# Expert choice and the first up stage as one program, with a budget for the splits and 54 candidate pairs

## The chip, the cores and the metric

One core of a Trainium2 chip runs the whole kernel. The metric is the device time of one execution in microseconds. The page calls TensorE PE, VectorE DVE, ScalarE ACT, GpSimd POOL and SyncE SP.

## The reference, cut to what matters

Two blocks of two layers each work on 256 tokens of width 1024 in float32. The change touches only the expert layer (`peer_ffn`) of the second block, twice in an execution:

```python
q = (xc @ w_q).reshape(c, 8, 2, 128)
sc = jnp.einsum('chpd,hpnd->chpn', q, sub_keys)         # 8 heads, 2 halves, 128 keys each
top_s, top_i = lax.top_k(sc, 16)
cand_s = top_s[:, :, 0, :, None] + top_s[:, :, 1, None, :]      # 16 x 16 sums a head
cand_i = top_i[:, :, 0, :, None] * 128 + top_i[:, :, 1, None, :]
best_s, best_j = lax.top_k(cand_s.reshape(c, 8, 256), 16)
idx = jnp.take_along_axis(cand_i.reshape(c, 8, 256), best_j, axis=-1)
gate = jax.nn.softmax(best_s, axis=-1)
act = jax.nn.gelu(jnp.einsum('chkd,cd->chk', u_tab[idx], xc), approximate=False)
out = jnp.einsum('chk,chkd->cd', gate * act, v_tab[idx])
```

There are 128 x 128 experts with a row in `u_tab` and in `v_tab` each. Both lists of 16 are sorted, so the pair of the i-th best first and the j-th best second key (counted from 0) can be among the best 16 sums only where (i + 1)(j + 1) <= 16. The kernel before ignores this and selects among all 256 sums.

## The kernel before

**Dense experts.** The kernel gathers nothing. It multiplies the tokens by all of `u_tab` (the up stage, in two halves of 64 tiles of 128 experts: `up0` and `up1`), takes gelu of each, multiplies by a dense matrix of gates, and multiplies by all of `v_tab` (the down stage). A tile of 128 experts is one piece of 512 KB, loaded by SyncE into `w_raw` (four slots).

**Splits.** Each float32 weight is split in two parts for TensorE. A piece has two halves k = 2T and 2T + 1 for tile T. ScalarE copies a half to `w_hi` (`split_hi`, L182). VectorE subtracts it from the raw one to get `w_lo` (`split_lo`, L191). In `up0` VectorE does only the even halves and GpSimd the odd ones (`split_lo_too`, L200); each waits for the split before its own, so that the order of `w_lo_done` holds. `w_hi` and `w_lo` have four slots of one half each. TensorE then issues 12 matmuls a half (`col_half`, L224 to L226), 24 a tile, and ScalarE takes the gelu of each finished tile (L2667), which SyncE stores to HBM (L2610).

**Order in ScalarE's queue.** `UpPhase.scalar` splits both halves of tile T and then takes the gelu of tile T - 1. The two PSUM banks of the up products alternate, so TensorE's tile T waits for the gelu of tile T - 2.

**The choice.** `choose_experts` (L2914) is three programs (`nc.Block`), each of which ends on all engines before the next begins. The first is 64 matmuls of queries and keys on TensorE (L2946) and eight copies on ScalarE (L2955). The second runs `up0` on SyncE, TensorE, ScalarE and GpSimd, and the selection on VectorE: the best 16 of 128 keys in `top16` (MAX8 at L2997 and L3004, FIND_INDEX8 at L3000 and L3007, MATCH_REPLACE8 at L3001), two rows at a time; all 256 sums of a head (L3022) and `top16` over them; then the picks, which compare each chosen position with 0..15 in a tile of 128 x 16 (L3042), multiply by the key indices (L3046) and add up (L3050). VectorE's splits stand among these: `link` puts in one split at every second call and then waits for the operation before it. At the end ScalarE takes Exp of the scores (L3066) and VectorE normalizes (L3056 to L3060). The third program, `turn_heads`, transposes the three results (L847) and copies them to `chosen` (L855, L863). Then `up1` begins as a fourth program, in which VectorE makes one-hot rows out of `chosen`, does both halves of each split, and GpSimd none.

Of the kernel before, what the change touches and what calls it, by code (L numbers as in the profile page):

```python
# [2574 lines left out]
def passes(eng, body, rounds, peel_first=1, peel_last=False):  # L2575


    for n in range(peel_first):
        body(n)
    with eng.Fori(peel_first, rounds - peel_last) as n:  # L2580
        body(n)
    if peel_last:
        body(rounds - 1)
# [32 lines left out]
class UpPhase:  # L2616
# [41 lines left out]
    def scalar(self, act, gates=None):  # L2658
# [22 lines left out]
        passes(act, body, self.ROUNDS, peel_first=1 if self.which else 2)  # L2681
# [231 lines left out]

def choose_experts(K, qT, keys, iota16, chosen, phase):  # L2914
# [8 lines left out]
    V = nc.vector  # L2923
    with ExitStack() as ctx:
# [4 lines left out]
        topf = sb("top_index_f", [P, TT, HP, TOPK])  # L2929
        best = sb("best_scores", [P, TT, PH, TOPK])  # L2930
        bj = sb("best_index", [P, TT, PH, TOPK], U32)
        part = sb("best_part", [P, TT, 2, HK], U32)
        partf = sb("best_part_f", [P, TT, 2, HK])
        res = sb("chosen_rows", [P, TT, 3, HK])
        sm = sb("gate_sums", [P, TT, PH])
        exp_done = K.sem("gate_exp")
        scored, copied = K.sem("keys_scored"), K.sem("keys_copied")
        with ExitStack() as c2:
            ps = K.ps("key_scores_ps", [P, TT, HP // 4, 4, NK], c2)
            with nc.Block() as block:  # L2940
                @block.tensor
                def _(pe):
                    for t in range(TT):
                        for g in range(HP // 4):
                            for i in range(4):
                                ins = nc.tensor.matmul(ps[:, t, g, i, :], qT[:, 4 * g + i, t * P:(t + 1) * P],  # L2946
                                                       keys[:, 4 * g + i, :], start=True, stop=True)
                            ins.then_inc(scored, 1)

                @block.scalar  # L2950
                def _(act):
                    for t in range(TT):
                        for g in range(HP // 4):
                            act.wait_ge(scored, (HP // 4) * t + g + 1)
                            nc.scalar.activation(sc[:, t, 4 * g:4 * g + 4, :], ps[:, t, g], ACT.Copy).then_inc(copied, 1)  # L2955
        K.half_filled = 0

        def fill(dve):

            if K.half_filled < 2 * HALF:  # L2960

                if K.half_filled % 2 == 0:
                    K.split_lo(dve, phase.k0 + K.half_filled, in_turn=True)
                K.half_filled += 1

        def link(dve, ins):

            ins.then_inc(K.dve.sem, 1)
            K.dve.n += 1
            fill(dve)  # L2970
            dve.wait_ge(K.dve.sem, K.dve.n)

        with ExitStack() as c2:
            phase.take_banks(c2)
            rest = K.sb("scores_rest", [P, 2, NK], F32, c2)
            cand = K.sb("candidates", [P, 2, TOPK * TOPK], F32, c2)
            crest = K.sb("candidates_rest", [P, 2, TOPK * TOPK], F32, c2)
            eq = K.sb("picked", [P, HK, TOPK], F32, c2)
            with nc.Block() as block:
                @block.sync  # L2980
                def _(sp):
                    phase.sync(sp)

                @block.tensor
                def _(pe):
                    passes(pe, lambda n: [phase.tensor_tile(pe, j, n) for j in range(BODY)], phase.ROUNDS)

                @block.gpsimd
                def _(pool):
                    passes(pool, lambda n: [K.split_lo_too(pool, phase.k0 + 2 * j + 1, rep=n) for j in range(BODY)],  # L2990
                           phase.ROUNDS)

                def top16(dve, jobs):


                    for src, spare, v, i in jobs:
                        ins = V.max(v[:, 0:8], src)  # L2997
                    link(dve, ins)
                    for src, spare, v, i in jobs:
                        V.max_index(i[:, 0:8], v[:, 0:8], src)  # L3000
                        ins = V.match_replace(spare, v[:, 0:8], src, NEG_MAX)  # L3001
                    link(dve, ins)
                    for src, spare, v, i in jobs:
                        ins = V.max(v[:, 8:16], spare)  # L3004
                    link(dve, ins)
                    for src, spare, v, i in jobs:
                        ins = V.max_index(i[:, 8:16], v[:, 8:16], spare)  # L3007
                    return ins

                @block.vector  # L3010
                def _(dve):
                    for t in range(TT):
                        for g in range(HP // 2):
                            link(dve, top16(dve, [(sc[:, t, 2 * g + u, :], rest[:, u, :], top[:, t, 2 * g + u, :],
                                                   topi[:, t, 2 * g + u, :]) for u in range(2)]))
                    K.dve.link(dve, V.tensor_copy(topf[:], topi[:]))
                    for t in range(TT):
                        tv = top[:, t].rearrange("p (h a) k -> p h a k", a=2)
                        for h in range(0, PH, 2):
                            for u in range(2):  # L3020

                                ins = V.tensor_tensor(cand[:, u].rearrange("p (a b) -> p a b", a=TOPK),  # L3022
                                                      bcast_last(tv[:, h + u, 0, :], TOPK),
                                                      bcast_mid(tv[:, h + u, 1, :], TOPK), ALU.add)
                            link(dve, ins)
                            link(dve, top16(dve, [(cand[:, u], crest[:, u], best[:, t, h + u], bj[:, t, h + u])
                                                  for u in range(2)]))
                    for t in range(TT):
                        ins = V.tensor_tensor(res[:, t, 2, :].rearrange("p (h k) -> p h k", h=PH), best[:, t],
                                              bcast_last(best[:, t, :, 0], TOPK), ALU.subtract)  # L3030
                    ins.then_inc(exp_done, 1)
                    for t in range(TT):
                        flat = bj[:, t].rearrange("p h k -> p (h k)")
                        V.tensor_scalar(part[:, t, 0, :], flat, 4, None, ALU.logical_shift_right)
                        ins = V.tensor_scalar(part[:, t, 1, :], flat, 15, None, ALU.bitwise_and)
                    link(dve, ins)
                    link(dve, V.tensor_copy(partf[:], part[:]))
                    for t in range(TT):
                        tf = topf[:, t].rearrange("p (h a) k -> p h a k", a=2)
                        for a in range(2):  # L3040

                            link(dve, V.tensor_tensor(eq[:], bcast_last(partf[:, t, a, :], TOPK),  # L3042
                                                      bcast_mid(iota16, HK), ALU.is_equal))
                            for h in range(PH):
                                e = eq[:, h * TOPK:(h + 1) * TOPK, :]
                                ins = V.tensor_tensor(e, e, bcast_mid(tf[:, h, a, :], TOPK), ALU.mult)  # L3046
                                if h % 4 == 3:
                                    fill(dve)
                            link(dve, ins)
                            link(dve, V.tensor_reduce(res[:, t, a, :], eq[:], AX.X, ALU.add))  # L3050
                    while K.half_filled < 2 * HALF:
                        fill(dve)
                    dve.wait_ge(exp_done, 2)
                    g4 = lambda t: res[:, t, 2, :].rearrange("p (h k) -> p h k", h=PH)
                    for t in range(TT):
                        ins = V.tensor_reduce(sm[:, t, :], g4(t), AX.X, ALU.add)  # L3056
                    link(dve, ins)
                    link(dve, V.reciprocal(sm[:], sm[:]))
                    for t in range(TT):
                        V.tensor_tensor(g4(t), g4(t), bcast_last(sm[:, t, :], TOPK), ALU.mult)  # L3060

                @block.scalar
                def _(act):
                    phase.scalar(act)
                    act.wait_ge(exp_done, 1)
# [310 lines left out]
```

## Time and profile before

| | |
|---|---|
| median of 3 runs | 2782.22 us |
| lowest, highest | 2779.45, 2785.15 us |
| the profiled execution, its own time | 2781.84 us |
| its span | 2780.1 us |
| TensorE busy | 94% |
| VectorE busy | 74% |
| ScalarE busy | 54% |
| GpSimd busy | 8% |
| mean granted TensorE clock | 0.979 of full |

The span is what the profiler saw between the first and the last instruction; the execution's own time is what the metric counts. A share is an average over stages with different limits.

### The profile page before, as it was taken

How to read it: one execution, taken by the hardware profiler on the slowest of the kernel's cores; microseconds unless marked ns; L12 is line 12 of the kernel's file. 1: busy time of each engine (PE TensorE's matmuls, PEld its weight loads, DVE VectorE, ACT ScalarE, POOL GpSimd, SP SyncE). 2: the span in 40 equal slices, each digit the busy share in tenths (PEclk: the TensorE clock that was granted, in tenths of full speed). 3: DMA queues.
4: the chain of work that ended last, by engine and by line, in shares of the span. 5: the costliest groups of instructions: out<-in, count | busy, mean ns of one | idle time of the engine just before them, and what ended most of it. 6: DMA issues, size and time to landing. Idle time of an engine off the chain costs nothing. (4 is left out here: it accounts for less than half of the span.)

```text
span 2780.1 us, 56603 instructions
## 1 busy us (share of the span) xinstructions
PE 2620.0 (94%) x17192; PEld 2375.4 (85%) x17192; DVE 2045.2 (74%) x4601; ACT 1500.0 (54%) x2975; POOL 222.3 (8%) x172
## 2 busy tenths in 40 slices
PE   7989999989988999799999999989998999999997
PEld 6869988779976999799988888778998999888886
DVE  5767767767768569877767777786589777777777
ACT  6555555654555445466655555555454566555554
POOL 0000000000000044200000000000344000000000
PEclk9999999999999999999999999989999999999999
DMA  5226654236543477455567777625576555577775
GB/s 203 84 72 182 183 175 139 79 123 187 182 158 121 148 228 227 158 173 176 173 209 242 241 240 242 204 90 175 176 227 190 161 176 173 182 241 242 239 243 183
DMA packets 194609, 503.48 MB, mean 181 GB/s; under 512 B 22608, under 2 KB 88400, under 8 KB 193104
## 3 DMA queue, kind: packets, MB, share of 16 engines
q1 hardware_dynamic: 194512, 502.28, 57.4%
q8 instruction: 50, 0.82, 0.1%
q14 instruction: 47, 0.39, 0.0%
HBM read 467.59 MB, written 34.60 MB: 181 GB/s over the span
## 5 line engine op out<-in xcount | busy, mean ns | idle before, releaser
L191 DVE TENSOR_TENSOR w_lo<-w_raw,w_hi 128x512 fp32r<-128x512 f32 (+1 forms) x1432 | 975.8, 685 | 355.5 <-ACT w_hi L182 335.4
L182 ACT ACTIVATE w_hi<-w_raw 128x512 fp32r<-128x512 f32 (+2 forms) x1592 | 926.4, 621 | 179.3 <-PE banks_right L226 137.9
L224 PE MATMUL up_up<-hT_hi,w_hi 128*128 128x256 f32 x2048 | 596.4, 291 | 26.6 <-DVE w_lo L191 20.5
L225 PE MATMUL up_up<-hT_lo,w_hi 128*128 128x256 f32 x2048 | 582.1, 284 | 0.0
L226 PE MATMUL up_up<-hT_hi,w_lo 128*128 128x256 f32 x2048 | 582.0, 284 | 0.0
L224 PEld LDWEIGHTS up_up<-hT_hi,w_hi 128*128 128x128 f32 x2048 | 395.2, 193 | 31.2 <-DVE w_lo L191 23.9
L236 PE MATMUL banks_left<-w_hi,expert_hi 128*128 128x512 f32 x1008 | 393.7, 391 | 7.7 <-DVE w_lo L191 7.7
L225 PEld LDWEIGHTS up_up<-hT_lo,w_hi 128*128 128x128 f32 x2048 | 395.9, 193 | 0.0
L226 PEld LDWEIGHTS up_up<-hT_hi,w_lo 128*128 128x128 f32 x2048 | 395.1, 193 | 0.0
L237 PE MATMUL banks_left<-w_lo,expert_hi 128*128 128x512 f32 x1008 | 393.2, 390 | 0.0
L238 PE MATMUL banks_left<-w_hi,expert_lo 128*128 128x512 f32 x1008 | 393.1, 390 | 0.0
L200 POOL TENSOR_TENSOR w_lo<-w_raw,w_hi 128x512 fp32r<-128x512 f32 (+1 forms) x160 | 214.0, 1338 | 1941.6 <-POOLq L2895 608.7
L224 PE MATMUL banks_right<-hT_hi,w_hi 128*128 128x256 f32 x1120 | 325.9, 291 | 8.2 <-DVE hT_lo L573 2.9
L225 PE MATMUL banks_right<-hT_lo,w_hi 128*128 128x256 f32 x1120 | 320.8, 286 | 0.0
L226 PE MATMUL banks_right<-hT_hi,w_lo 128*128 128x256 f32 x1120 | 320.7, 286 | 0.0
L2667 ACT ACTIVATE expert_gelu<-up_up 128x256 f32<-128x256 f32 x256 | 98.4, 384 | 403.0 <-PE up_up L226 403.0
L2744 ACT ACTIVATE expert_hi<-gates 128x256 fp32r (+1 forms) x256 | 106.9, 418 | 323.6 <-PE banks_left L238 320.9
L224 PEld LDWEIGHTS banks_right<-hT_hi,w_hi 128*128 128x128 f32 x1120 | 218.8, 195 | 14.8 <-issue 5.9
L236 PEld LDWEIGHTS banks_left<-w_hi,expert_hi 128*128 128x128 f32 x1008 | 190.0, 189 | 47.5 <-DVE expert_lo L2760 8.1
L237 PEld LDWEIGHTS banks_left<-w_lo,expert_hi 128*128 128x128 f32 x1008 | 190.1, 189 | 39.6
L238 PEld LDWEIGHTS banks_left<-w_hi,expert_lo 128*128 128x128 f32 x1008 | 189.9, 188 | 39.3
L2760 DVE TENSOR_TENSOR expert_lo<-gates,expert_hi 128x256 fp32r<-128x256 f32 x256 | 109.0, 426 | 154.3 <-ACT expert_hi L2744 154.3
(400 smaller groups left out, 3890.8 us busy)
## 6 DMA issues: line engine op xcount, KB each, us to landing
w_raw<-in_peer_u_c SPq DMA_DIRECT2D x256, 512.0 KB, 3.5
w_raw<-in_peer_v SPq DMA_DIRECT2D x256, 512.0 KB, 3.5
w_raw<-in_w_up_c SPq DMA_DIRECT2D x88, 512.0 KB, 3.6
expert_gelu_held<-expert_gelu SPq DMA_DIRECT2D x256, 128.0 KB, 1.7
expert_back<-expert_gelu_held SPq DMA_DIRECT2D x256, 128.0 KB, 3.2
w_raw<-in_w_down SPq DMA_DIRECT2D x44, 512.0 KB, 4.1
w_raw<-in_w_in_r SPq DMA_DIRECT2D x40, 512.0 KB, 3.6
w_raw<-in_w_in_c SPq DMA_DIRECT2D x32, 512.0 KB, 3.6
```

The source lines that it names most:

```text
L182: self.nc.scalar.activation(self.w_hi[:, k % SLOTS, 0:width], self.raw_half(k, width), ACT.Copy).then_inc(self.sem("w_hi_done"), 1)
L191: self.nc.vector.tensor_tensor(self.w_lo[:, k % SLOTS, 0:width], self.raw_half(k, width), self.w_hi[:, k % SLOTS, 0:width].bitcast(F32), A ...
L200: self.nc.gpsimd.tensor_tensor(self.w_lo[:, k % SLOTS, 0:width], self.raw_half(k, width), self.w_hi[:, k % SLOTS, 0:width].bitcast(F32), A ...
L224: self.nc.tensor.matmul(bank, hi, self.hT_hi[:, c, :], start=(c == 0), stop=False)
L225: self.nc.tensor.matmul(bank, hi, self.hT_lo[:, c, :], start=False, stop=False)
L226: last = self.nc.tensor.matmul(bank, lo, self.hT_hi[:, c, :], start=False, stop=(c == DC - 1))
L236: self.nc.tensor.matmul(bank, act_hi[:, cols], hi, start=start, stop=False)
L237: self.nc.tensor.matmul(bank, act_hi[:, cols], lo, start=False, stop=False)
L238: last = self.nc.tensor.matmul(bank, act_lo[:, cols], hi, start=False, stop=stop)
L2667: K.nc.scalar.activation(shelf.out[:, j, :], self.up[:, j % 2, 0:SEQ], ACT.Gelu).then_inc(self.gelu_done, 1)
L2744: K.nc.scalar.activation(self.hi[:, j % 2, :], tile_of(self.gates, j + BODY * n), ACT.Copy).then_inc(self.hi_done, 1)
L2760: self.K.nc.vector.tensor_tensor(self.lo[:, j % 2, :], tile_of(self.gates, j + BODY * n), self.hi[:, j % 2, :].bitcast(F32), ALU.subtract) ...
```

## The change

The first two programs of `choose_experts` and the transposes become one program, beside `up0`:

- TensorE computes the scores of tokens 0 to 127, tile 0 of `up0`, the scores of tokens 128 to 255 in the same banks (each group after ScalarE's copy of the first), and then the other tiles. Ahead of tile 63 it waits for the gates and does the six transposes.
- ScalarE copies the scores after the splits of tile 0 and, for the second half, after those of tile 1 and the first gelu. Exp stands behind the gelu of tile 55, in the iteration of tile 56.
- VectorE's splits are placed by a budget (`Paced`): each operation counts 0.13 us + width/950, and a split is put in as soon as 1.9 us are reached, behind the operation that was just issued and ahead of the wait for it. After the picks the splits up to the 58th (tile 57) follow, then the normalization, then the last six, and the copies to `chosen`.
- `top16` works on four rows at a time. The second selection works on 54 sums a head, laid out in five segments (rows 0; 1; 2 to 3; 4 to 7; 8 to 15 with 16, 8, 5, 3, 1 columns). The place of a chosen one among the 54 is turned into row and column by 20 operations on 128 x 256.
- The picks become 16 times `(part == k) * index[k]` on 128 x 512 (scalar_tensor_tensor) and 15 additions, each waiting for the one before.
- `passes` can leave out more than one last iteration of the loop; ScalarE peels two and TensorE one.

The removed lines are those of the program above.

```diff
@@ -2579,8 +2579,8 @@
         body(n)
     with eng.Fori(peel_first, rounds - peel_last) as n:
         body(n)
-    if peel_last:
-        body(rounds - 1)
+    for n in range(rounds - peel_last, rounds):
+        body(n)
 def is_first(n):
@@ -2655,7 +2655,7 @@
         for j in range(BODY):
             store(j, self.ROUNDS - 1)
-    def scalar(self, act, gates=None):
+    def scalar(self, act, gates=None, also={}, peel_last=0):
         K, k0, shelf = self.K, self.k0, self.shelf
         def gelu(j, n):
@@ -2678,7 +2678,9 @@
                     gates.move(act, j - 2, n)
                 elif gates and not is_first(n):
                     gates.move(act, j + 2, n - 1)
-        passes(act, body, self.ROUNDS, peel_first=1 if self.which else 2)
+                if isinstance(n, int) and (n, j) in also:
+                    also[n, j]()
+        passes(act, body, self.ROUNDS, peel_first=1 if self.which else 2, peel_last=peel_last)
         gelu(BODY - 1, self.ROUNDS - 1)
         if gates:
             for j in (2, 3):
@@ -2911,6 +2913,43 @@
     phase.end()
+class Paced:
+    def __init__(self, K, dve, phase, each):
+        self.K, self.dve, self.k0, self.each = K, dve, phase.k0, each
+        self.spent, self.filled = 0.0, 0
+    def fill(self):
+        if self.filled < HALF:
+            self.K.split_lo(self.dve, self.k0 + 2 * self.filled, in_turn=True)
+            self.filled += 1
+    def fill_to(self, count):
+        while self.filled < count:
+            self.fill()
+    def spend(self, width, ops=1):
+        self.spent += ops * (0.13 + width / 950)
+        while self.spent >= self.each:
+            self.spent -= self.each
+            self.fill()
+    def link(self, ins, width, ops=1):
+        self.K.dve.mark(ins)
+        self.spend(width, ops)
+        self.K.dve.settle(self.dve)
+SEGMENTS = [(0, 1, 16), (1, 2, 8), (2, 4, 5), (4, 8, 3), (8, 16, 1)]
+CAND_N = sum((b - a) * w for a, b, w in SEGMENTS)
+FIRST_OF_ROW = [0, 16, 24, 29, 34, 37, 40, 43, 46]
+assert all(any(a <= i < b and j < w for a, b, w in SEGMENTS) for i in range(TOPK) for j in range(TOPK) if (i + 1) * (j + 1) <= TOPK)
 def choose_experts(K, qT, keys, iota16, chosen, phase):
@@ -2921,152 +2960,165 @@
     NEG_MAX = -3.0e38
     HK = PH * TOPK
     V = nc.vector
+    EXP_AT, TAIL = (phase.ROUNDS - 2, 0), 58
     with ExitStack() as ctx:
         sb = lambda n, s, d=F32: K.sb(n, s, d, ctx)
         sc = sb("key_scores", [P, TT, HP, NK])
         top = sb("top_scores", [P, TT, HP, TOPK])
         topi = sb("top_index", [P, TT, HP, TOPK], U32)
...
+        topf = sb("top_index_f", [P, TT, 2, PH, TOPK])
         best = sb("best_scores", [P, TT, PH, TOPK])
         bj = sb("best_index", [P, TT, PH, TOPK], U32)
...
+        partf = sb("best_part_f", [P, TT, 2, PH, TOPK])
+        term = sb("picked_term", [P, TT, 2, PH, TOPK])
+        picked = sb("picked", [P, TT, 2, PH, TOPK])
+        gate = sb("chosen_gates", [P, TT, HK])
         sm = sb("gate_sums", [P, TT, PH])
...
+        rest = sb("scores_rest", [P, 4, NK])
+        cand = sb("candidates", [P, TT, PH, CAND_N])
+        crest = sb("candidates_rest", [P, 4, CAND_N])
+        pos = sb("best_position", [P, TT, PH, TOPK])
+        row, line, first = (sb(f"best_{n}", [P, TT, PH, TOPK]) for n in ("row", "line", "first"))
+        scored, copied, exp_done, ready, turned = (
+            K.sem(n) for n in ("keys_scored", "keys_copied", "gate_exp", "chosen_ready", "chosen_turned"))
+        phase.take_banks(ctx)
+        ps = K.ps("key_scores_ps", [P, HP // 4, 4, NK], ctx)
+        tps = K.ps("chosen_ps", [P, 4, SEQ], ctx)
+        with nc.Block() as block:
+            @block.sync
+            def _(sp):
+                phase.sync(sp)
+            @block.tensor
+            def _(pe):
+                def scores(t):
+                    for g in range(HP // 4):
+                        if t:
+                            pe.wait_ge(copied, g + 1)
+                        for i in range(4):
+                            ins = nc.tensor.matmul(ps[:, g, i, :], qT[:, 4 * g + i, t * P:(t + 1) * P],
+                                                   keys[:, 4 * g + i, :], start=True, stop=True)
+                        ins.then_inc(scored, 1)
+                def turn():
+                    pe.wait_ge(ready, 1)
+                    for j in range(3):
+                        for t in range(TT):
+                            src = gate[:, t, :] if j == 2 else picked[:, t, j]
+                            ins = nc.tensor.transpose(tps[:, j, t * P:(t + 1) * P], src, K.ident[:])
+                        if j:
+                            ins.then_inc(turned, 1)
+                def body(n):
+                    for j in range(BODY):
+                        if isinstance(n, int) and n == phase.ROUNDS - 1 and j == BODY - 1:
+                            turn()
+                        phase.tensor_tile(pe, j, n)
+                        if is_first(n) and j == 0:
+                            scores(1)
+                scores(0)
+                passes(pe, body, phase.ROUNDS, peel_last=1)
+            @block.gpsimd
+            def _(pool):
+                passes(pool, lambda n: [K.split_lo_too(pool, phase.k0 + 2 * j + 1, rep=n) for j in range(BODY)],
+                       phase.ROUNDS)
+            @block.scalar
+            def _(act):
+                def copies(t):
+                    for g in range(HP // 4):
+                        act.wait_ge(scored, (HP // 4) * t + g + 1)
+                        nc.scalar.activation(sc[:, t, 4 * g:4 * g + 4, :], ps[:, g], ACT.Copy).then_inc(copied, 1)
+                def gates():
+                    act.wait_ge(exp_done, 1)
+                    nc.scalar.activation(gate[:], gate[:], ACT.Exp).then_inc(exp_done, 1)
+                phase.scalar(act, also={(0, 0): lambda: copies(0), (0, 1): lambda: copies(1), EXP_AT: gates}, peel_last=2)
+            @block.vector
+            def _(dve):
+                pace = Paced(K, dve, phase, 1.9)
+                link = pace.link
+                def top16(jobs):
+                    n = jobs[0][0].shape[-1]
                     for src, spare, v, i in jobs:
                         ins = V.max(v[:, 0:8], src)
...
+                    link(ins, n, len(jobs))
                     for src, spare, v, i in jobs:
                         V.max_index(i[:, 0:8], v[:, 0:8], src)
                         ins = V.match_replace(spare, v[:, 0:8], src, NEG_MAX)
...
+                    link(ins, n + 70, 2 * len(jobs))
                     for src, spare, v, i in jobs:
                         ins = V.max(v[:, 8:16], spare)
...
+                    link(ins, n, len(jobs))
                     for src, spare, v, i in jobs:
                         ins = V.max_index(i[:, 8:16], v[:, 8:16], spare)
...
+                    link(ins, n + 70, len(jobs))
+                pace.fill()
+                for t in range(TT):
+                    for g in range(0, HP, 4):
+                        dve.wait_ge(copied, (HP // 4) * t + g // 4 + 1)
+                        top16([(sc[:, t, g + u, :], rest[:, u, :], top[:, t, g + u, :], topi[:, t, g + u, :])
+                               for u in range(4)])
+                for t in range(TT):
+                    ins = V.tensor_copy(topf[:, t].rearrange("p a h k -> p h a k"), topi[:, t].rearrange("p (h a) k -> p h a k", a=2))
+                link(ins, 256, 2)
+                for t in range(TT):
+                    tv = top[:, t].rearrange("p (h a) k -> p h a k", a=2)
+                    c0 = 0
+                    for a, b, w in SEGMENTS:
+                        n = (b - a) * w
+                        ins = V.tensor_tensor(cand[:, t, :, c0:c0 + n].rearrange("p h (a b) -> p h a b", b=w),
+                                              bcast_last(tv[:, :, 0, a:b], w), bcast_mid(tv[:, :, 1, 0:w], b - a), ALU.add)
+                        pace.spend(PH * n)
+                        c0 += n
+                K.dve.link(dve, ins)
+                for t in range(TT):
+                    for h in range(0, PH, 4):
+                        top16([(cand[:, t, h + u], crest[:, u], best[:, t, h + u], bj[:, t, h + u]) for u in range(4)])
+                for t in range(TT):
+                    ins = V.tensor_tensor(gate[:, t].rearrange("p (h k) -> p h k", h=PH), best[:, t],
+                                          bcast_last(best[:, t, :, 0], TOPK), ALU.subtract)
+                ins.then_inc(exp_done, 1)
+                pace.spend(128, 2)
+                link(V.tensor_copy(pos[:], bj[:]), 256)
+                link(V.tensor_scalar(line[:], pos[:], FIRST_OF_ROW[8] - 1.0, 0.0, ALU.subtract, ALU.max), 256)
+                for s in FIRST_OF_ROW[1:8]:
+                    src = line if s == FIRST_OF_ROW[1] else row
+                    link(V.scalar_tensor_tensor(row[:], pos[:], float(s), src[:], ALU.is_ge, ALU.add), 256)
+                for i, (a, b, w) in enumerate(SEGMENTS):
+                    c = float(FIRST_OF_ROW[a] - w * a)
+                    link(V.tensor_scalar((line if i else first)[:], row[:], float(w), c, ALU.mult, ALU.add), 256)
+                    if i:
+                        link(V.tensor_tensor(first[:], first[:], line[:], ALU.min), 256)
+                V.tensor_copy(partf[:, :, 0], row[:])
+                link(V.tensor_tensor(partf[:, :, 1], pos[:], first[:], ALU.subtract), 256, 2)
+                flat = lambda x: x.rearrange("p t a h k -> p (t a h) k")
+                value = lambda k: bcast_last(flat(topf)[:, :, k], TOPK)
+                for k in range(TOPK):
+                    dst = term if k else picked
+                    link(V.scalar_tensor_tensor(flat(dst), flat(partf), float(k), value(k), ALU.is_equal, ALU.mult), 512)
+                    if k:
+                        link(V.tensor_tensor(picked[:], picked[:], term[:], ALU.add), 512)
+                pace.fill_to(TAIL)
+                dve.wait_ge(exp_done, 2)
+                g4 = lambda t: gate[:, t, :].rearrange("p (h k) -> p h k", h=PH)
+                for t in range(TT):
+                    ins = V.tensor_reduce(sm[:, t, :], g4(t), AX.X, ALU.add)
+                link(ins, 128, 2)
+                link(V.reciprocal(sm[:], sm[:]), 16)
+                for t in range(TT):
+                    ins = V.tensor_tensor(g4(t), g4(t), bcast_last(sm[:, t, :], TOPK), ALU.mult)
+                ins.then_inc(ready, 1)
+                pace.fill_to(HALF)
+                for i in range(2):
+                    dve.wait_ge(turned, i + 1)
+                    rows = slice(2 * i, min(2 * i + 2, 3))
+                    V.tensor_copy(chosen[:, rows, :], tps[:, rows, :])
+        phase.end()
 def second_layer(K, l, cols, table, after, entry, following):
```

## Rows read from the trace of the kernel before

**Rows 1.** The page, part 1: busy us, share of the span, instructions.
```profile
PE 2620.0 (94%) x17192; PEld 2375.4 (85%) x17192; DVE 2045.2 (74%) x4601; ACT 1500.0 (54%) x2975; POOL 222.3 (8%) x172
```

**Rows 2.** Stretches, first layer: window, length, busy us of each engine; clock, DMA.
```profile
963.35:1117.80 154.45, 154.38 (x1272) 154.17 (x1272) 123.54 (x459) 77.27 (x160) 68.77 (x53) 0.99 0.71 222
1117.80:1160.60 42.80, 34.27 (x264) 32.49 (x264) 39.46 (x51) 14.80 (x31) 18.17 (x11) 1.00 0.50 159
```

**Rows 3.** TensorE's timeline at both edges: start, length, operation, idle before it.
```profile
953.50 7.38 PE L2946 MATMUL key_scores_ps<-sub_keys,peer_qT 128*128 128x128 f32 x64 [0.78 <-PEq L618]
963.35 0.43 PE L224 MATMUL up_up<-hT_hi,w_hi 128*128 128x256 f32 x1 [2.46 <-DVE w_lo L191]
...
966.98 0.28 PE L226 MATMUL up_up<-hT_hi,w_lo 128*128 128x256 f32 x1
...
1160.32 0.28 PE L226 MATMUL up_up<-hT_hi,w_lo 128*128 128x256 f32 x1
1164.38 1.01 PE L847 MATMUL chosen_ps<-ident,chosen_rows 128*128 128x128 f32 x6 [3.78 <-PEq L2979]
1167.62 0.58 PE L224 MATMUL up_up<-hT_hi,w_hi 128*128 128x256 f32 x1 [2.23 <-DVE w_lo L191]
```

**Rows 4.** ScalarE's timeline at both edges and at tile 53, SyncE's last stores.
```profile
960.92 0.60 ACT L2955 ACTIVATE key_scores<-key_scores_ps 128x512 f32<-128x512 f32 x1 [0.30 <-PE key_scores_ps L2946]
961.86 2.19 ACT L182 ACTIVATE w_hi<-w_raw 128x512 fp32r<-128x512 f32 x4 [0.34 <-PEq L2940]
...
968.01 0.39 ACT L2667 ACTIVATE expert_gelu<-up_up 128x256 f32<-128x256 f32 x1 [2.66 <-PE up_up L226]
...
1117.76 0.38 ACT L2667 ACTIVATE expert_gelu<-up_up 128x256 f32<-128x256 f32 x1 [1.37 <-PE up_up L226]
...
1160.64 0.38 ACT L2667 ACTIVATE expert_gelu<-up_up 128x256 f32<-128x256 f32 x1 [2.52 <-PE up_up L226]
1161.04 1.28 ACT L3066 ACT_TABLE_LOAD   x1
1162.33 0.42 ACT L3066 ACTIVATE chosen_rows<-chosen_rows 128x256 f32<-128x256 f32 x1
...
1159.25 2.13 SPq L2610 DMA_DIRECT2D expert_gelu_held<-expert_gelu  x4
```

**Rows 5.** Waits, 1116 to 1162, then 2114 to 2162: total us, times, longest.
```profile
PE up_up L224 <- DVE w_lo L191: 5.5, 6, 2.0
PE up_up L224 <- POOL w_lo L200: 3.1, 2, 1.5
...
PE up_up L224 <- DVE w_lo L191: 5.6, 6, 2.0
```

**Rows 6.** VectorE's and GpSimd's timelines in the picks, VectorE's ahead of `up1`.
```profile
1114.59 3.27 DVE L3042 TENSOR_TENSOR picked<-best_part_f,iota 128x2048 f32<-128x2048 f32 x1
1117.78 0.68 DVE L191 TENSOR_TENSOR w_lo<-w_raw,w_hi 128x512 fp32r<-128x512 f32 x1
1118.38 3.87 DVE L3046 TENSOR_TENSOR picked<-picked,top_index_f 128x256 f32<-128x256 f32 x8
...
1125.57 2.28 DVE L3042 TENSOR_TENSOR picked<-best_part_f,iota 128x2048 f32<-128x2048 f32 x1
...
1166.87 0.69 DVE L191 TENSOR_TENSOR w_lo<-w_raw,w_hi 128x512 fp32r<-128x512 f32 x1 [1.02 <-ACT w_hi L182]
...
1114.38 1.33 POOL L200 TENSOR_TENSOR w_lo<-w_raw,w_hi 128x512 fp32r<-128x512 f32 x1 [1.66 <-DVE w_lo L191]
1118.62 1.34 POOL L200 TENSOR_TENSOR w_lo<-w_raw,w_hi 128x512 fp32r<-128x512 f32 x1 [2.91 <-DVE w_lo L191]
...
1125.80 3.16 POOL L200 TENSOR_TENSOR w_lo<-w_raw,w_hi 128x512 fp32r<-128x512 f32 x1 [1.50 <-DVE w_lo L191]
```

**Rows 7.** VectorE's groups by form (first layer's choice): busy us, mean ns; one line's instructions.
```profile
L3000 DVE FIND_INDEX8 top_index<-top_scores,key_scores 128x8 uint32<-128x128 f32 x32 | 9.1, 286 | 0.0
...
L473 DVE SCALAR_TENSOR_TENSOR x<-x,banks_right x8: 632/680/689, 890.6 to 1894.5; 128x512 f32<-128x512 f32 x8
```

More of the change, by code:

```diff
@@ L2928, in choose_experts @@
         topi = sb("top_index", [P, TT, HP, TOPK], U32)
-        topf = sb("top_index_f", [P, TT, HP, TOPK])
+        topf = sb("top_index_f", [P, TT, 2, PH, TOPK])
         best = sb("best_scores", [P, TT, PH, TOPK])
         bj = sb("best_index", [P, TT, PH, TOPK], U32)
-        part = sb("best_part", [P, TT, 2, HK], U32)
-        partf = sb("best_part_f", [P, TT, 2, HK])
-        res = sb("chosen_rows", [P, TT, 3, HK])
+        partf = sb("best_part_f", [P, TT, 2, PH, TOPK])
+        term = sb("picked_term", [P, TT, 2, PH, TOPK])
@@ L2935, in choose_experts @@
+        picked = sb("picked", [P, TT, 2, PH, TOPK])
+        gate = sb("chosen_gates", [P, TT, HK])
         sm = sb("gate_sums", [P, TT, PH])
[L2936 to L2993, printed above, removed]
@@ L2996, in top16 @@
                     for src, spare, v, i in jobs:
                         ins = V.max(v[:, 0:8], src)
-                    link(dve, ins)
+                    link(ins, n, len(jobs))
                     for src, spare, v, i in jobs:
@@ L3001, in top16 @@
                         ins = V.match_replace(spare, v[:, 0:8], src, NEG_MAX)
-                    link(dve, ins)
+                    link(ins, n + 70, 2 * len(jobs))
                     for src, spare, v, i in jobs:
                         ins = V.max(v[:, 8:16], spare)
-                    link(dve, ins)
+                    link(ins, n, len(jobs))
                     for src, spare, v, i in jobs:
                         ins = V.max_index(i[:, 8:16], v[:, 8:16], spare)
-                    return ins
@@ L3010, in _ @@
[L3010 to L3065, printed above, removed]
-                    nc.scalar.activation(res[:, :, 2, :], res[:, :, 2, :], ACT.Exp).then_inc(exp_done, 1)
-            phase.end()
-        with ExitStack() as c2:
-            turn_heads(K, c2, "chosen", [(lambda t, j=j: res[:, t, j, :]) for j in range(3)], chosen)
+                    link(ins, n + 70, len(jobs))
[5 more added lines that the diff above has]
+                               for u in range(4)])
```

## The prediction

> **What bounds the kernel now.** I read the page's busy shares first: TensorE is busy 94% of the span [rows 1], so only stretches in which it stands still or runs slow can be won. The stretches by engine show where, in the choice with the first up stage of the first of two equal layers: up to 1117.8 us it never stands still, and from there to 1160.6 us it is busy 34.3 of 42.8 us while VectorE is nearly full [rows 2]. Then TensorE's timeline for the edges [rows 3], ScalarE's and SyncE's for the steps between two programs [rows 4], the waits for the late stretch [rows 5], and the timelines of VectorE and GpSimd there [rows 6].
>
> From the first key score (953.50) to the first matmul of the second up stage (1167.62) are 214.1 us [rows 3]. They add up so:
> - key scores: 7.38.
> - 960.88 to 963.35, waiting for the first split: 2.47.
> - After that pause the matmuls come 0.21 apart, at 1.2 GHz; the eighteenth (966.98) is the first at 0.12, 2.4 GHz: 3.63 us for what takes 17 x 0.12 = 2.04, so 1.59 lost.
> - 64 tiles of 24 matmuls at 0.12: 184.3. The gelus, one a tile, confirm it: 52 periods from 968.01 to 1117.76 are 2.88 each [rows 4].
> - the last 11 periods, 1117.76 to 1160.64, are 42.88 instead of 31.68: 11.2 lost, waiting for w_lo from VectorE and GpSimd [rows 5].
> - last matmul issued by 1160.44, next stage at 1167.62: 7.18 (last gelu, a program's end, Exp, the gate sums, a program's end, transposes of 1.01, again an end, first split).
> Sum 214.1. The second layer waits the same [rows 5].
>
> **What the change takes away, per layer.** Key scores of the first half run at once, and the split of tile 0 beside them: VectorE and GpSimd have 3.7 us for 0.7 + 1.3 [rows 6]. The second half's scores follow tile 0, whose 2.88 us cover ScalarE's copies. So the 2.47 go, and with no pause ahead of tile 0 its 1.59 too. The scores' own 7.38 stay on TensorE. Exp and gate sums leave the end. What is left after the last tile: last matmul's issue to gelu's end 0.20 + 0.38, SyncE's store issue 0.34 (its row ends 1161.38, the gelu 1161.02), the program's end 0.34 (961.52 to 961.86), first w_hi to w_lo 0.66, w_lo to matmul 0.75 (1166.87 to 1167.62) [rows 3, 4, 6]: 2.7, against 7.18, and the six transposes now stand ahead of tile 63 as 1.01 more. The slow start of the second up stage stays, since 2.5 us of pause were enough for it at 963.35. Gone: 2.47 + 1.59 + 7.18 - 2.7 - 1.0 = 7.5. Gone too, if the splits are in time: the 11.2. Together 18.7.
>
> The 54 candidates instead of 256, the four jobs a step and the new arithmetic cost or save nothing by themselves: until 1117.8 TensorE didn't wait for VectorE. They matter through when a split is late.
>
> **When a split is late.** In steady state the w_hi of tile T+1 is done about 1.1 us after tile T-1 ends (0.20 to the gelu, its 0.38, w_hi 2.19/4 = 0.55 [rows 4]) and VectorE's split must start by 2.88 - 0.69 - 0.07 = 2.1. VectorE may so be 1.0 us late. The program puts a split behind each 1.9 us of its own estimate, 0.13 + width/950 an operation (below: the budget), a split takes 0.60 (1117.78 to 1118.38 [rows 6]): 2.5 of 2.88, which looks safe. First selection: 32 rows of two MAX8, two FIND_INDEX8 and a replace over 128, five records, each read as the 0.286 of a FIND [rows 7], 1.43 x 32 = 46 us at most, against a budget of 8 groups x 6.18 = 49.4, so 26 splits: 46 + 26 x 0.6 = 62 us beside 75 us of TensorE. It is covered, and without that cover each us late would be a us lost. Over 54 the 16 rows take between 54/128 of that and the same, 10 to 23 us; with 9.7 splits 16 to 29 beside 28 us, and I take 22, since part of each is fixed. At joints, where eight FIND and replace operations stand between two splits (8 x 0.286 = 2.3 us at most), I put 0.5 us.
>
> The rest of the selection is another kind of work. The index arithmetic is 20 operations on 256 elements, the picks 16 + 15 on 512, nearly all with two inputs in SBUF, and GpSimd does the other half of each split. The rows say that these exclude each other: the 2048-wide comparison takes 2.28 us alone but 3.27 where a GpSimd split had begun; a GpSimd split that came while it ran took 3.16 instead of 1.33; eight multiplications by 256 took 3.87 where by width they are worth 2.28, and a GpSimd split is most of the difference [rows 6]. So a tile costs VectorE 0.60 (split) + 1.33 (GpSimd) + the budget's operations. By the budget a pick is 0.669, so 2.84 of them a split. A two-input operation of 512 records 0.68 (read from a scalar_tensor_tensor of that width whose one input was in PSUM [rows 7]), and each waits for the one before. With one of three starting while GpSimd waits its turn I take 0.65 each: 1.85. Sum 3.78, 0.90 more than 2.88. The picks' budget, 31 x 0.669 = 20.7, is 10.9 splits: 9.8 us lost. The index part, 20 x 0.40 = 8.0 us of budget, is 4.2 splits: 3.8, less the 1.0 that VectorE may be late, less 1.0 as an estimate for its operations with one input, which are worth less than budgeted: 1.8. Sum 11.6. The added waits (one after nearly each operation) hold up only what is in that sum: the next split, hence GpSimd's, hence TensorE.
>
> The Trainium skill states the rule that this speaks for: SBUF — State Buffer, section "SBUF: two separate sides", has VectorE's operations with two SBUF inputs and GpSimd's share a port pair as an exclusive lock, held for the whole instruction. The trace agrees (3.16 for 1.33). By 1.9 + 0.6 < 2.88 alone the change would look free of late splits; by the rule it is not.
>
> Exp in the middle: after gelu 55 ScalarE loads a table and does Exp, 1162.33 - 1161.04 + 0.42 = 1.71 us [rows 4]; tile 57's split is that much later, less 1.0 of slack: 0.7 lost. The gelu table's reload, 1.29, fits: ScalarE works 1.5 of each 2.88. Bounds 0 to 2. VectorE and the transposes aren't late: budget 100 us / 1.9 = 53 splits, so the picks end near tile 54, and the gates are due before tile 63, 17 us of margin even after waiting for Exp in tile 56.
>
> The Trainium skill, ScalarE: Activation LUTs, section "What ACT_TABLE_LOAD costs", adds a drain of about 1.38 us to the load's 1.28. The trace shows 1.29 from load to Exp, with the engine already empty; by the page this step would lose 1.4 us more a layer, and the estimate would be 2773.
>
> **Sum.** Lost anew: 11.6 + 0.5 + 0.7 = 12.8 of 18.7. Won 5.9 a layer, 11.8 in two. The profiled execution took 2781.8 (span 2780.1), 0.4 below the median 2782.2, so I leave that aside: 2770. Unknown ends: the picks' loss from 0 (no exclusion for scalar_tensor_tensor, short waits) to 18 (each 0.2 us dearer and GpSimd 0.3 later); joints 0 to 2. If only some terms err, 2762 to 2777.
>
> **Rivals.**
> A. The splits are in time after all: the picks are chained with gaps, and GpSimd works in them or isn't excluded by the new operation. Then only 0.7 to 2 are lost, 17 to 18 won a layer: 2747. For it: the rows show only operations in unbroken series or 2048 wide, and no scalar_tensor_tensor beside GpSimd. Against: the 3.16 and 3.87, and that the other half of the picks are additions of the kind shown.
> B. Slower. GpSimd doesn't get its turn between two operations of VectorE but after three: its half comes 1.83 later (3.16 - 1.33), so TensorE waits some 1.8 us in each of 15 tiles: 27 + 1.2 lost against 18.7, 19 slower in two layers: 2801. It decides from 1.2 us a tile on. Against: at 1118.62 GpSimd began after the first of eight multiplications with no gap between them [rows 6].
> C. The picks are dearer than read (each add and compare 0.2 us longer): 31 x 0.2 = 6.2 more a layer and nothing is left: 2781, no change.
>
> **How the numbers follow.** Forecast 0.62, A 0.2, C 0.1, B 0.08. The range holds the forecast's 2762 to 2777 and most of A, and leaves out B and the lowest of A: 2748 to 2779. A measurement here tells 0.2%, 5.6 us, from no change. Faster by more: the forecast's (less 0.05 for its upper end) and A's, and nothing of C: 0.78 to 0.84, taken as 0.82. Within: 0.1. Slower: 0.08.
>
> **What would show it.** TensorE: no pause between scores and tile 0, matmuls 0.12 apart from the start; about 2.7 us between up stages. Gelu periods of 2.88 up to about tile 38, then near 3.8 for some 12 tiles, 2.88 again with one longer by 0.7 at tile 57. GpSimd's split records near 1.8 in the picks. If the periods stay 2.88 there, A holds; if they pass 4.1, B or C. The forecast is wrong also if a wait stands ahead of the transposes.

## The result and the profile after

The changed kernel takes 2762.14 us (median of 4 runs, 2759.4 to 2765.01), the kernel before 2780.9 beside it. The ratio is 0.9926, 95% interval 0.9914 to 0.9938: faster by 0.6% to 0.9%. The forecast was 2770, 11.8 us won; 18.8 were. The profiled execution is the slowest of the four: 2765.01, span 2763.2.

TensorE's timeline at the edges of the first layer's stage, as in [rows 3]:

```profile
956.74 3.81 PE L2999 MATMUL key_scores_ps<-sub_keys,peer_qT 128*128 128x128 f32 x32 [0.78 <-PEq L618]
960.31 0.36 PE L224 MATMUL up_up<-hT_hi,w_hi 128*128 128x256 f32 x1
960.51 0.28 PE L225 MATMUL up_up<-hT_lo,w_hi 128*128 128x256 f32 x1
960.63 0.28 PE L226 MATMUL up_up<-hT_hi,w_lo 128*128 128x256 f32 x1
...
963.27 3.74 PE L2999 MATMUL key_scores_ps<-sub_keys,peer_qT 128*128 128x128 f32 x32
...
1154.39 0.60 PE L3008 MATMUL chosen_ps<-ident,picked 128*128 128x128 f32 x4
1154.82 0.38 PE L3008 MATMUL chosen_ps<-ident,chosen_gates 128*128 128x128 f32 x2
1160.74 0.39 PE L224 MATMUL up_up<-hT_hi,w_hi 128*128 128x256 f32 x1 [2.67 <-DVE w_lo L191]
```

No pause stands between the scores and tile 0, and its matmuls come 0.12 apart from the start. From the first score to the next up stage are 204.0 us, 214.1 before. (That the stage begins 3.2 later than before is not the change's: it was there before any changed instruction ran. From the first gelu of the second up stage to the next layer's first score it is 0.9 longer as well, 781.3 instead of 780.4. So the two profiled spans differ by 16.9 only, though the two layers' stages give more.)

ScalarE's timeline: a late stretch, Exp, the last gelu:

```profile
969.91 0.38 ACT L2667 ACTIVATE expert_gelu<-up_up 128x256 f32<-128x256 f32 x1 [1.24 <-PE up_up L226]
...
1073.61 0.38 ACT L2667 ACTIVATE expert_gelu<-up_up 128x256 f32<-128x256 f32 x1 [1.46 <-PE up_up L226]
...
1124.87 0.38 ACT L2667 ACTIVATE expert_gelu<-up_up 128x256 f32<-128x256 f32 x1 [1.41 <-PE up_up L226]
...
1133.51 0.38 ACT L2667 ACTIVATE expert_gelu<-up_up 128x256 f32<-128x256 f32 x1 [1.46 <-PE up_up L226]
1133.91 1.28 ACT L3035 ACT_TABLE_LOAD   x1
1135.20 0.42 ACT L3035 ACTIVATE chosen_gates<-chosen_gates 128x256 f32<-128x256 f32 x1
1135.53 1.13 ACT L182 ACTIVATE w_hi<-w_raw 128x512 fp32r<-128x512 f32 x2
1136.68 1.28 ACT L2667 ACT_TABLE_LOAD   x1
...
1140.18 0.38 ACT L2667 ACTIVATE expert_gelu<-up_up 128x256 f32<-128x256 f32 x1 [0.78 <-PE up_up L226]
...
1158.11 0.38 ACT L2667 ACTIVATE expert_gelu<-up_up 128x256 f32<-128x256 f32 x1 [3.14 <-PE up_up L226]
```

These are the gelus of tiles 1, 37, 52, 55, 57 and 63. The time from one gelu to the next is what a tile takes on TensorE, 2.88 where nothing is late. Read as such periods: 36 of 2.88 on average; 15 that take 51.26 instead of 43.20, so 8.06 lost; 3 of 2.88; two that take 6.67 instead of 5.76 around Exp, 0.91 lost; 5 of 2.88; and the last, with the transposes, 3.53, 0.65 more.

VectorE's timeline in the picks, and GpSimd's beside it, to be held against [rows 6]:

```profile
1089.36 0.69 DVE L191 TENSOR_TENSOR w_lo<-w_raw,w_hi 128x512 fp32r<-128x512 f32 x1
1089.97 0.69 DVE L3105 TENSOR_TENSOR picked<-picked,picked_term 128x512 f32<-128x512 f32 x1
1090.69 1.67 DVE L3103 SCALAR_TENSOR_TENSOR picked_term<-best_part_f,top_index_f 128x512 f32<-128x512 f32 x1
1092.39 0.69 DVE L3105 TENSOR_TENSOR picked<-picked,picked_term 128x512 f32<-128x512 f32 x1
1093.00 0.69 DVE L191 TENSOR_TENSOR w_lo<-w_raw,w_hi 128x512 fp32r<-128x512 f32 x1
...
1090.21 1.60 POOL L200 TENSOR_TENSOR w_lo<-w_raw,w_hi 128x512 fp32r<-128x512 f32 x1 [2.04 <-DVE w_lo L191]
```

After each of VectorE's splits one operation of the picks runs alone at 0.69, and the next takes 1.67, whichever of the two operations it is: it stands behind GpSimd's split. That split's record is longer too (1.60 instead of 1.30): it began while the first operation ran.

### The profile page after: what moved, and what is told of

It is laid out like the page before. It is cut to its first block and busy times, and to the rows that moved or that the text cites. A ratio compares the mean times of both kernels' runs of the same rounds, so it can differ in the third digit from the quotient of the medians.

```text
span 2763.2 us, 56517 instructions
## 1 busy us (share of the span) xinstructions
PE 2627.0 (95%) x17192; PEld 2379.1 (86%) x17192; DVE 2002.3 (72%) x4605; ACT 1498.3 (54%) x2973; POOL 222.1 (8%) x172
## 5 line engine op out<-in xcount | busy, mean ns | idle before, releaser
L224 PE MATMUL up_up<-hT_hi,w_hi 128*128 128x256 f32 x2048 | 596.5, 291 | 12.2 <-DVE w_lo L191 10.9
L225 PEld LDWEIGHTS banks_right<-hT_lo,w_hi 128*128 128x128 f32 x1120 | 219.3, 196 | 2.1
```

Source lines behind the costliest of these rows:

```text
L224: self.nc.tensor.matmul(bank, hi, self.hT_hi[:, c, :], start=(c == 0), stop=False)
L225: self.nc.tensor.matmul(bank, hi, self.hT_lo[:, c, :], start=False, stop=False)
```

## Experiments

Each was timed beside the kernel before, and the ratios are to that kernel. The changed kernel's own, from another series, is 0.9926 (0.9914 to 0.9938), so its distance to one of these kernels is known to some 5 us either way.

| | median us | ratio (95%) |
|---|---|---|
| selection alone | 2773.1 | 0.9969 (0.9957 to 0.9981) |
| edges alone | 2765.7 | 0.9951 (0.9937 to 0.9965) |
| picks in PSUM | 2747.78 | 0.9877 (0.9862 to 0.9892) |
| two budgets | 2743.69 | 0.9865 (0.9849 to 0.9880) |
| odd halves on VectorE | 2747.38 | 0.9876 (0.9860 to 0.9891) |
| all 256 candidates | 2762.11 | 0.9927 (0.9913 to 0.9940) |
| two budgets and PSUM | 2743.24 | 0.9859 (0.9844 to 0.9874) |
| Exp after the splits | 2741.62 | 0.9853 (0.9838 to 0.9868) |

**The selection alone.** The new selection in the old three programs.

```diff
-        phase.take_banks(ctx)                       # scores, up stage and transposes in one program
+        with nc.Block() as block: ...               # all scores and copies first
+        phase.take_banks(c3)                        # then the up stage with the new selection
...
-                pace.fill_to(TAIL)
+                pace.fill_to(HALF)                  # Exp and gate sums after the last tile
...
+            turn_heads(K, c2, "chosen", [(lambda t, j=j: src(t, j)) for j in range(3)], chosen)
```

> The new selection with its budget, but in the three programs of the kernel before (scores, up stage, transposes), Exp and gate sums after the last tile. Theory 1 (most of the gain comes from the edges between programs, the selection gives 11.2 - 8.1 = 3.1 us a layer): 2780.9 - 6 = 2775. Rival (the new selection is the larger part and would give the 11.2 back by itself): below 2765.

2773.1. TensorE's timeline has the old edges again:

```profile
954.02 7.38 PE L2991 MATMUL key_scores_ps<-sub_keys,peer_qT 128*128 128x128 f32 x64 [0.78 <-PEq L618]
963.87 0.43 PE L224 MATMUL up_up<-hT_hi,w_hi 128*128 128x256 f32 x1 [2.46 <-DVE w_lo L191]
...
1161.83 0.90 PE L847 MATMUL chosen_ps<-ident,picked 128*128 128x128 f32 x4 [3.78 <-PEq L3003]
```

The late periods are those of the changed kernel (3.4 to 3.7 for tiles 40 to 51). In this profile the way from the first score to the second stage's first gelu (1170.08) is 216.1 against 219.1 before (1172.61): 3.1 a layer, 6 in two, inside the interval of the time (5 to 12 us). Theory 1 stands.

**The edges alone.** One program with the old selection.

```diff
-                pace = Paced(K, dve, phase, 1.9)
+                def fill(dve): ...                  # a split at every second call, as before
-                cand = sb("candidates", [P, TT, PH, CAND_N])
+                cand = sb("candidates", [P, 2, TOPK * TOPK])
...
+                        link(dve, V.tensor_tensor(eq[:], bcast_last(partf[:, t, a, :], TOPK), ...))
```

> One program as in the changed kernel (scores around tile 0, Exp in tile 56, transposes ahead of tile 63), with the selection of the kernel before: 256 candidates, 2048-wide comparisons, a split at every second call. Theory 1: the edges are worth 2.47 + 1.59 + 7.18 - 2.83 - 0.65 - 0.9 = 6.9 us a layer, so 2767, with the last eleven periods still 11 us too long. Rival (the edges only move the wait, the selection must be shorter for it): 2775 or more.

2765.7. The waits of TensorE from 1105 to 1158 are the old ones of [rows 5], and a new one: the picks end so late that the transposes wait.

```profile
PE up_up L224 <- DVE w_lo L191: 5.8, 7, 2.0
PE up_up L224 <- POOL w_lo L200: 3.1, 2, 1.5
PE chosen_ps L3006 <- DVE chosen_rows L3122: 1.5, 1, 1.5
```

The first score and the second stage's first gelu:

```profile
951.12 3.81 PE L2997 MATMUL key_scores_ps<-sub_keys,peer_qT 128*128 128x128 f32 x32 [0.78 <-PEq L618]
...
1164.00 0.39 ACT L2667 ACTIVATE expert_gelu<-up_up 128x256 f32<-128x256 f32 x1 [3.90 <-PE up_up L226]
```

That is 212.9 instead of 219.1: the edges alone give 6.2 in this layer (6.5 in the second), less than the 6.9 expected. The last eleven periods lose 13.8 here, where the 11.2 of before with the terms expected for Exp and the transposes would be 12.8; the wait ahead of the transposes is the new part of it. In the changed kernel the same way is 208.6, so the change gives 10.5 a layer by this measure: 6.2 from the edges alone, 3.1 from the selection alone, and 1.2 that only both together give. The wait of 1.5 for late picks, which the new selection takes away, is large enough for that. Theory 1 holds in the main, and the rival (2775 or more) falls.

**The picks in PSUM.** Same operations, but each reads only one of its inputs from SBUF; the additions write their sum to PSUM as well.

```diff
-                value = lambda k: bcast_last(flat(topf)[:, :, k], TOPK)
+                value = lambda k: bcast_last(flat_ps(0)[:, :, k], TOPK)      # key indices in a bank of the scores
...
-                    dst = term if k else picked
+                    dst = flat(term) if k else flat_ps(1)                     # running sum in the next bank
```

> The changed kernel with the key indices and the running sum of the picks in PSUM, so that each of the 31 operations has only one input in SBUF; same operations, widths, waits and budget. Theory 1 (the late splits come from the port that operations with two SBUF inputs and GpSimd's split exclude each other from): GpSimd's split no longer stops VectorE, a tile of three picks costs 0.60 + 3 x 0.75 = 2.9, the picks lose 1 us instead of 7, so 2762 - 12 = 2750. Rival (VectorE is simply full: the budget of 1.9 with its waits is dearer than 2.28): nothing changes, 2762, or slower by PSUM's longer access, 2764.

2747.78, 14 us less than the changed kernel (12.2 of it by the profiles, between the first score and the second stage's first gelu, in both layers together). VectorE and GpSimd in the picks:

```profile
1091.98 0.68 DVE L191 TENSOR_TENSOR w_lo<-w_raw,w_hi 128x512 fp32r<-128x512 f32 x1
1092.58 0.68 DVE L3105 SCALAR_TENSOR_TENSOR picked_term<-best_part_f,key_scores_ps 128x512 f32<-128x512 f32 x1
1093.29 0.70 DVE L3107 TENSOR_TENSOR key_scores_ps<-key_scores_ps,picked_term 128x512 f32<-128x512 f32 x1
1094.03 0.69 DVE L3105 SCALAR_TENSOR_TENSOR picked_term<-best_part_f,key_scores_ps 128x512 f32<-128x512 f32 x1
1094.63 0.68 DVE L191 TENSOR_TENSOR w_lo<-w_raw,w_hi 128x512 fp32r<-128x512 f32 x1
...
1092.82 1.30 POOL L200 TENSOR_TENSOR w_lo<-w_raw,w_hi 128x512 fp32r<-128x512 f32 x1 [1.36 <-DVE w_lo L191]
```

No 1.67 is left, and GpSimd is back at 1.30: three picks and a split take 2.65 instead of 3.64. The index part, which stayed in SBUF, is the late stretch left (periods up to 3.5 for tiles 39 to 42); besides it one period is 3.80, that of tile 28, in the sums of the candidates, which have two SBUF inputs too. In all, late splits cost 2.7 in the first layer instead of 8.1. This shows the exclusion itself: nothing but the place of operands changed, and for scalar_tensor_tensor (L3105) only that of one input, since its result stayed in SBUF. The rival falls.

**Two budgets.** The exclusion stays, but the splits are spread for it: more work between two splits up to the second top 16, less in the index part and the picks, whose operations wait for GpSimd.

```diff
-                pace = Paced(K, dve, phase, 1.9)
+                pace = Paced(K, dve, phase, 2.3)
...
+                pace.each = 1.3
                 link(V.tensor_copy(pos[:], bj[:]), 256)
```

> The changed kernel with a budget of 2.3 us a split up to the end of the second top 16, and 1.3 behind it. Theory 1 (the operations with two SBUF inputs cost GpSimd's 1.0 us more a tile, the others don't): first part 2.3 x 0.86 + 0.6 = 2.6 us a tile, second part 1.3 x 1.07 + 0.6 + 1.0 = 3.0 against 2.88; nearly no late split, 7 us less a layer, 2748. Rival (the budget's place doesn't matter, VectorE's sum of work over the stage does, and it was already enough): 2762.

2743.69, 18 us less than the changed kernel. From tile 2 on all gelu periods are 2.88 on average, up to that of tile 55. TensorE's waits from 1070 to 1152 (the longer one is the next stage's first split):

```profile
PE up_up L224 <- DVE w_lo L191: 3.3, 2, 2.7
```

The rival falls: the sum of VectorE's work is the same, and only its place against the splits changed.

**Odd halves on VectorE from tile 40.**

```diff
             self.K.split_lo(self.dve, self.k0 + 2 * self.filled, in_turn=True)
+            if self.filled >= 40:
+                self.K.split_lo(self.dve, self.k0 + 2 * self.filled + 1)
...
-                       phase.ROUNDS)
+                       10)                          # GpSimd's rounds, of 4 tiles each
```

> The changed kernel, but from tile 40 of the first up stage on VectorE splits the odd halves too and GpSimd none. VectorE gets 24 x 0.6 us more work. Theory 1 (GpSimd's split takes the port from VectorE for 1.0 us a tile): a tile of the picks costs 0.60 + 0.60 + 2.84 x 0.72 = 3.25 instead of 3.6, so the loss falls by 0.35 in 12 tiles, 4 us a layer, 2754. Rival (GpSimd works beside VectorE at no cost to it, VectorE is too full by itself): 0.6 more a tile, 7 us a layer slower, 2777.

2747.38. VectorE does 14 us more work a layer and the kernel is 15 us faster. Its timeline:

```profile
1099.07 1.28 DVE L191 TENSOR_TENSOR w_lo<-w_raw,w_hi 128x512 fp32r<-128x512 f32 x2
1100.27 0.68 DVE L3107 TENSOR_TENSOR picked<-picked,picked_term 128x512 f32<-128x512 f32 x1
1100.99 0.69 DVE L3105 SCALAR_TENSOR_TENSOR picked_term<-best_part_f,top_index_f 128x512 f32<-128x512 f32 x1
1101.72 0.69 DVE L3107 TENSOR_TENSOR picked<-picked,picked_term 128x512 f32<-128x512 f32 x1
1102.33 1.29 DVE L191 TENSOR_TENSOR w_lo<-w_raw,w_hi 128x512 fp32r<-128x512 f32 x2
```

A tile of three picks costs 3.26, as expected 3.25; the 15 late periods lose 3.5 instead of 8.1. That is 9 us in two layers; 2.4 more are the faster start of the second up stage (last section), and the rest is within the interval. Theory 1 stands; its rival expected 2777.

**All 256 candidates.**

```diff
-        cand = sb("candidates", [P, TT, PH, CAND_N])
+        cand = sb("candidates", [P, PH, TOPK * TOPK])
...
-                link(V.tensor_scalar(line[:], pos[:], FIRST_OF_ROW[8] - 1.0, 0.0, ALU.subtract, ALU.max), 256)
+                V.tensor_scalar(part[:, :, 0], bj[:], 4, None, ALU.logical_shift_right)
```

> The changed kernel with all 256 sums as candidates (row and column of a chosen one by shift and mask, 3 operations instead of 20), everything else as it is. The budget counts 35.5 instead of 18.5 for the second selection, 3.3 for its sums and 1.5 for the index part instead of 8: some 5 splits more before the picks end, at tile 58. Theory 1 (54 candidates make room in the budget and nothing else): the index part's 2 us of late splits go, the wider sums with two SBUF inputs bring some back, 2762 plus or minus 3. Rival (54 candidates are needed): the picks run into the gates and the transposes wait, 2770 or more.

2762.11, the time of the changed kernel. The late periods only stand elsewhere (tiles 31, 42, 51 to 60). With this budget the 54 candidates bring nothing; they leave room, which the budget of 1.9 doesn't use. Whether two budgets would keep their gain with 256 candidates, no run shows.

**Two budgets and PSUM; Exp after the splits.** The edits of both remedies together (index part too), and then Exp moved ahead of the gelu:

```diff
                     K.split_hi(act, k0 + 2 * j + h, rep=n)
+                if isinstance(n, int) and n and (n, j) in also:
+                    also[n, j]()
                 if j > 0:
                     gelu(j - 1, n)
...
-                if isinstance(n, int) and (n, j) in also:
+                if isinstance(n, int) and (n, j) in also and n == 0:
```

> The two budgets, and picks and index part in PSUM as well. Theory 1: with two budgets no split was late any more in the traces but after Exp, so the second remedy finds nothing to remedy: as with two budgets alone, 2743 plus or minus 2. Rival (there are small losses left behind GpSimd in the other halves): 2740.

> As the kernel with two budgets and PSUM, and Exp of the gates in ScalarE's queue between the splits of tile 56 and the gelu of tile 55 instead of behind that gelu. Theory 1 (Exp costs because it holds up the next split, 0.9 us a layer): the split of tile 57 waits for a gelu that is 3 us late now, the gelu of 55 holds up TensorE's tile 57 and the splits behind it: 1 to 2 us a layer lost instead of 0.9, 2744. Rival (behind the splits there is more slack): 0.3 to 0.6 lost, 2742, not to be told apart in the time but in the periods of the gelus.

2743.24 and 2741.62: both like two budgets alone. The time alone would not tell 2743 from the rival's 2740, but the profiles do: from the first score to the second stage's first gelu are 199.33 with two budgets and 199.33 with PSUM as well. Where no split is late, the place of an operand is worth nothing. In the second the three periods around Exp take 9.40 instead of 8.64, 0.76 lost instead of 0.91: neither expectation has the size right, and in the time the two can't be told apart. The three kernels with two budgets are the fastest tried, 1.4% to 1.5% under the kernel before and 0.6% to 0.7% under the changed one.

## Why the prediction was right in kind and short in size

- *The edges, 7.5 a layer.* Right: 2.47 and 1.59 are gone, the end is 2.83 (1157.91 to 1160.74) instead of 7.18 (said: 2.7), the transposes cost 0.65 (said: 1.0). 7.8 by these terms (2.47 + 1.59 + 7.18 - 2.83 - 0.65).
- *Exp in the middle, 0.7.* 0.91: the slack was 0.8 of the 1.71, not 1.0. *Joints, 0.5.* None: 36 periods of 2.88. The load took 1.29 here too (1133.91 to 1135.20), with the gelu done just before; the drain that the Trainium skill adds (ScalarE: Activation LUTs, "What ACT_TABLE_LOAD costs") doesn't show.
- *A late split needs two inputs in SBUF and GpSimd.* Right: shown by the picks in PSUM and by the odd halves on VectorE. Rival A falls: scalar_tensor_tensor is stopped like any other. B falls: GpSimd gets in after one operation. C falls: an operation of the picks records 0.69, as read (0.68). A's price was 17 to 18 won a layer, 2746 to 2748, so the stated range from 2748 on did not hold most of A, as it was said to.
- *The step that was mis-sized* is the term "a tile costs VectorE 0.60 (split) + 1.33 (GpSimd) + the budget's operations", 3.78 in the picks. Measured are 3.45: eleven steps from split to split, 1085.73 to 1123.66, in 37.93 us, with 30 operations of the picks in them. GpSimd's record is 1.6 long there (said: near 1.8), but it stops VectorE for 1.67 - 0.69 = 0.98 only. The row of before had said so: 3.27 against 2.28 is 0.99 [rows 6], and I took the length of GpSimd's own record instead. The rest of the term was nearly right: an operation takes 0.72 from start to start where the next waits for it and 0.61 where a split follows, 0.69 on average instead of 0.65, but 2.73 of them stand in a tile and not 2.84. So 0.60 + 0.98 + 2.73 x 0.69 = 3.46. The picks lost 0.57 in 11 tiles, 6.2 instead of 9.8; the index part about 1.9, as said (1.8).
- *The sum.* Lost anew 8.1 + 0.9 of 18.7 and the 0.4 of the transposes back: 10.1 a layer, 20 in two by the profile, 18.8 (ratio: 17 to 24) by the times. Forecast: 5.9 and 11.8. Of the 4.2 a layer between them 3.6 are the picks' term; the joints give 0.5, the edges 0.3, and Exp takes 0.2. The time lies at the lower end of the 2762 to 2777 that the prediction gave if only some terms err.

The estimate by the Trainium skill's rule of the shared port (SBUF — State Buffer, "SBUF: two separate sides") was the one to follow: of 1.9 + 0.6 alone no split would have been late, and 15 periods were. That section of the Trainium skill has the port held for the whole instruction; by the blocked engine's records it was 0.98 of GpSimd's 1.3 to 1.6, and that number had to be taken from a row.

## What to carry to other kernels

A budget that spreads a short, urgent operation among long work must count the work in the time it takes beside the other engines, not alone: here one number for two kinds of work left 8 us a layer. Two numbers won them all back; one operand of the picks moved to PSUM won 5.4. A blocked engine's loss is read from the blocked engine's record less its undisturbed one, not from the length of the record that blocks. And a selection made shorter (54 for 256) wins nothing while the engine that sets the end, here TensorE, isn't waiting for its result.

## What the runs showed that I had not expected

- GpSimd's split of 128 x 512 records 1.30 but holds VectorE's two-input operations up for 0.98. A cast of 128 x 256 with one SBUF input is held up as well: `best_position` took 1.38 beside the GpSimd split that began at 1069.79, while two casts of that size took 0.49 together at 1037.78, where GpSimd's split (1038.02) began behind the first of them. Some 1.1 us are the wait, then, as an estimate from these rows.
- The second up stage's first tile. In the changed kernel, after 2.67 us of pause, the first ten matmuls begin within 1.2 us, mostly 0.12 apart (2.4 GHz), and from 1161.9 to 1165.1 they come 0.21 apart (1.2 GHz). With two budgets the pause is 2.67 too, but the matmuls stay 0.12 apart. The stretches' columns end with the granted clock (of full speed), the DMA share and GB/s; first the changed kernel, then two budgets:

```profile
1161.90:1165.10 3.20, 3.20 (x18) 3.20 (x16) 3.20 (x9) 0.00 (x0) 0.00 (x0) 0.51 0.44 125
...
1152.00:1155.00 3.00, 3.00 (x25) 2.85 (x25) 3.00 (x9) 0.56 (x2) 0.00 (x0) 1.00 0.12 22
```

From the last gelu of the first stage to the first of the second are 7.2 to 7.3 us in the changed kernel, the edges alone and all 256 candidates. In the four kernels with two budgets or with odd halves on VectorE they are 6.0, in both layers, and in the picks in PSUM 7.2 in one layer and 6.0 in the other. These 1.2 us a layer are part of what the experiments win beyond the late splits (2 x (8.1 + 1.2) = 18.6 for two budgets, 18.4 measured). What decides between the two is open: the pause doesn't tell them apart, the picks in PSUM show both in one execution, and that the 1.2 us come with the remedies is seen in these runs but not shown to be caused by them.
